# One hybrid decoder layer on one Trainium2 core: scoring in four steps, own token through TensorE, copies of the value results on ScalarE

## The reference

```python
q, k = rms_norm(q, g_q), rms_norm(k, g_k)
gate = einsum(q, mean of k over each block of 256)      # 8 past blocks
idx = top_k(gate, 3)                                     # ties: the lower block first
s_sel = q . k_sel / 8 - slope * distance                 # keys of the three blocks kept
s_own = q . k_own / 8                                    # the sample's own token
p = softmax(concat(s_sel, s_own))
o = p_sel @ v_sel + p_own @ v_own
attn = o @ w_attn_proj
```

## Time and profile before

| | |
|---|---|
| median of 3 runs | 666.08 us (663.58 to 670.77) |
| profiled execution | 667.34 us, span 665.6 us |
| busy in the span: PE, DVE, ACT, POOL | 566.9, 420.4, 240.2, 135.4 us |
| mean granted TensorE clock | 0.922 |

### The profile page before, as it was taken

The page is one execution under the profiler, slowest core; times in us unless marked ns, Lnnn a source line. Parts: engine busy times, 40 slices in busy tenths (PEclk is TensorE's granted clock), DMA queues, the critical chain, the costliest instruction groups (busy, mean ns, idle before and its releaser), DMA issues.

```text
span 665.6 us, 10279 instructions
## 1 busy us (share of the span) xinstructions
PE 566.9 (85%) x4080; PEld 463.0 (70%) x4080; DVE 420.4 (63%) x735; ACT 240.2 (36%) x438; POOL 135.4 (20%) x206
## 2 busy tenths in 40 slices
PE   4869998778778797868679597977999999999997
PEld 2657686546455554536446586966999999999997
DVE  2425793598797979887865366346655666664441
ACT  1102311454462727342135143136433344333341
POOL 8110100274746657661010000000000000000000
PEclk9969998798888887979988899976999999999999
DMA  8998297439896887898472739644775845466600
GB/s 264 384 413 311 73 406 245 160 127 387 285 401 254 348 330 279 342 373 349 162 296 85 261 130 391 225 133 148 232 254 191 286 158 182 120 173 175 176 34 33
DMA packets 85199, 159.30 MB, mean 239 GB/s; under 512 B 2572, under 2 KB 61112, under 8 KB 81047
## 3 DMA queue, kind: packets, MB, share of 16 engines
q1 hardware_dynamic: 79328, 89.27, 40.4%
q0 software_dynamic: 5120, 67.71, 25.7%
q10 hardware_dynamic: 703, 1.67, 0.7%
HBM read 156.39 MB, written 2.72 MB: 239 GB/s over the span
## 4 chain that ended last, share of the span: by engine, by line
PE 61%; DVE 15%; DMA 13%; POOL 4%; ACT 3%; issue 3%; ACTq 1%; SPq 1%; POOLq 0%; DVEq 0%
PE acc L1200 13%; PE acc L1291 12%; PE acc L1292 11%; PE acc L1293 11%; DMA kring<-in_cache_k,rowof 5%; PE chain L1376 4%; DVE prod L819 3%; DVE sall L826 3%; POOL cvT L471 3%; PE acc L1167 3%; DMA wring<-in_w_ada 2%; DMA wring<-in_w_out 2%; DMA wring<-in_w_attn_proj 1%; DMA wring<-in_w_ffn_in 1%; DVE wlo L896 1%
## 5 line engine op out<-in xcount | busy, mean ns | idle before, releaser
L1200 PE MATMUL acc<-hT,wring 128*128 128x264 f32 x576 | 158.8, 430 | 3.7 <-DVE hT L785 1.9
L896 DVE TENSOR_TENSOR wlo<-wring,whi 128x1024 fp32r<-128x1024 f32 (+2 forms) x92 | 101.9, 1108 | 93.2 <-ACT whi L499 92.5
L1200 PEld LDWEIGHTS acc<-hT,wring 128*128 128x128 f32 x576 | 116.5, 210 | 36.7 <-issue 13.5
L1291 PE MATMUL acc<-xlo,whi 128*128 128x264 f32 x416 | 123.9, 298 | 13.5 <-DVE xT L1070 7.4
L499 ACT ACTIVATE whi<-wring 128x1024 fp32r<-128x1024 f32 (+2 forms) x92 | 88.2, 963 | 119.4 <-PE acc L1293 94.3
L1292 PE MATMUL acc<-xhi,wlo 128*128 128x264 f32 x416 | 120.9, 291 | 0.0
L1293 PE MATMUL acc<-xhi,whi 128*128 128x264 f32 x416 | 120.9, 291 | 0.0
L471 POOL TENSOR_TENSOR cvT<-cvT,cprod 128x256 f32<-128x256 f32 x120 | 88.2, 735 | 86.6 <-ACT cprod L499 71.3
L1291 PEld LDWEIGHTS acc<-xlo,whi 128*128 128x128 f32 x416 | 81.2, 195 | 18.2 <-DVE wlo L896 8.6
L819 DVE TENSOR_TENSOR prod<-kring,qbc 128x1024 f32<-128x1024 f32 x64 | 77.4, 1210 | 7.5 <-DMA kring<-in_cache_k,rowof 3.3
L1292 PEld LDWEIGHTS acc<-xhi,wlo 128*128 128x128 f32 x416 | 81.7, 197 | 0.1
(11 more groups left out here) (221 smaller groups left out, 623.5 us busy)
## 6 DMA issues: line engine op xcount, KB each, us to landing
wring<-in_w_ada SPq DMA_DIRECT2D x24, 1024.0 KB, 8.2
wring<-in_w_ffn_in SPq DMA_DIRECT2D x22, 1024.0 KB, 6.8
wring<-in_w_in SPq DMA_DIRECT2D x12, 1024.0 KB, 19.1
wring<-in_w_ffn_out SPq DMA_DIRECT2D x16, 704.0 KB, 5.8
wring<-in_w_out SPq DMA_DIRECT2D x4, 1024.0 KB
wring<-in_w_in SPq DMA_DIRECT2D x6, 512.0 KB, 14.3
wring<-in_w_in SPq DMA_DIRECT2D x4, 768.0 KB, 12.2
wring<-in_w_conv_proj SPq DMA_DIRECT2D x2, 1024.0 KB, 15.7
```

Source lines behind the costliest of these rows:

```text
L896: v.tensor_tensor(wlo[:, place, 0:n, :], w, whi[:, place, 0:n, :].bitcast(F32), ALU.subtract)\
L1200: ins = mm(bank[:, 0:R], w[:, k, P * t:P * t + P], src[:, k, :], start=k == 0, stop=k == KD - 1)
L1291: mm(bank[:, 0:R], whi[:, place, k - k0, :], lo[:, k, :], start=k == 0, stop=False)
```

## The change

It was announced as: scoring in four steps, own token through TensorE, copies behind the value matmuls on ScalarE, value matmuls in the next sample's turn, third key place. The diff does this:

- Scoring goes in 4 steps of 4 pages (`STEPS` = 4), so `multiply` and `add_up` have 2048 elements each; steps 0 and 1 read the first half of the keys, 2 and 3 the second. The steps are placed anew between the softmax steps: step 0 stands ahead of the copy that opens the turn.
- The three comparisons and one sum that rank the blocks become a subtraction and two fused instructions.
- The own token's values go through TensorE: the value rows of the samples are kept as rows (`vrow`, partitions 32 to 39), DVE makes an 8 x 8 weight `pown`, and one more matmul adds it to the value result. The products and sums of the own token on DVE go.
- The weights of the value matmuls are no longer padded (`pg`, 8 columns for 32). The result lies in `chain` alone, which is cleared once; all other small results lie in a bank `small`, and the prompt's output shares a bank with its turned rows.
- ScalarE copies the value result out of PSUM unmasked (`pvm`); the head is chosen by the turned copies, whose second operand is `headof`. ScalarE also writes them to `oT`. Both stand behind the copy of the prompt's output in its queue. TensorE does the turned copies behind the next prompt scores.
- The scalings of the prompt's exponentials move from DVE to ScalarE, behind the second portion of tap products. The ring of tap products has 4 places for 5.
- On TensorE the first gate tile is finished before the turned rows, and the sum of the exponentials stands ahead of the prompt's value matmuls. The query of `b+2` is spread in turn `b`.
- The last turn does the convolution's SiLU and split ahead of the copy of the value result.

```diff
-STEPS = 8
...
-CONV_RING = 5
+CONV_RING = 4
...
+                tap_products(b, 1)
+                act.wait_ge(prin_ready, b + 1)
+                for t, (c0, c1) in enumerate(((0, P), (P, 384))):
+                    func(pr[:, c0:c1], pr[:, c0:c1], ACT.Copy, scale=prin[:, t:t + 1]).then_inc(pn_ready, 1)
                 act.wait_ge(pt_ready, b + 1)
                 act.wait_ge(pp_ready, b)
                 func(prT[:, :], psT[:, 0:384], ACT.Copy).then_inc(pc_ready, 1)
-                tap_products(b, 1)
...
+                if b == B - 1:
+                    conv_rows()
+                act.wait_ge(v_used, CH * (b + 1))
+                func(pvm[:, :], pv[:, :], ACT.Copy).then_inc(pvm_ready, 1)
+                act.wait_ge(pv_ready, b + 1)
+                for e in range(2):
+                    rows = slice(DH * e, DH * e + DH)
+                    func(oT[rows, :, S + b], pvT[rows, e:H:2], ACT.Copy).then_inc(o_ready, 1)
...
+                multiply_next(0)
                 dve.wait_ge(gs_ready, b + 1)
-                v.tensor_copy(gsT[:, :], chain[:, 0:QU]).then_inc(gst_ready, 1)
+                v.tensor_copy(gsT[:, :], sums_).then_inc(gst_ready, 1)
+                add_up_next(0)
...
-                at_same = mark(v.tensor_tensor(cmp1[:, :, :], gm, gn, ALU.is_equal))
-                at_higher = mark(v.tensor_tensor(cmp2[:, :, :], gm, gn, ALU.is_gt))
-                dve.wait_ge(dve_step, at_same)
-                at_first = mark(v.tensor_tensor(cmp1[:, :, :], cmp1[:, :, :], lower[0:H, :, :], ALU.mult))
+                at_less = mark(v.tensor_tensor(cmp1[:, :, :], gm, gn, ALU.subtract))
...
+                dve.wait_ge(dve_step, at_less)
+                at_first = mark(v.scalar_tensor_tensor(cmp2[:, :, :], cmp1[:, :, :], 0.0, lower[0:H, :, :],
+                                                       ALU.is_equal, ALU.mult))
...
+                at_count = mark(v.scalar_tensor_tensor(cmp2[:, :, :], cmp1[:, :, :], 0.0, cmp2[:, :, :],
+                                                       ALU.is_gt, ALU.add))
...
-                multiply_next(0)
+                multiply_next(1)
...
-                add_up_next(0)
...
                 v.tensor_reduce(m1, s1[:, :, :].rearrange("p g h -> p h g"), AX.X, ALU.max).then_inc(m1_ready, 1)
-                multiply_next(1)
+                add_up_next(1)
                 if j == 0 and i + 1 < CT:
                     gated_glu(i + 1)
-                add_up_next(1)
+                dve.wait_ge(pe_ready, 2 * b + 2)
+                v.reciprocal(prin, psum_).then_inc(prin_ready, 1)
...
                 v.tensor_scalar(dg, ident[0:H, 0:H], nmx, None, ALU.mult).then_inc(dg_ready, 1)
-
-                dve.wait_ge(dve_step, at_prin)
-                at_pn = mark(v.tensor_scalar(pr[:, 0:P], pr[:, 0:P], prin[:, 0:1], None, ALU.mult))
-                dve.wait_ge(dve_step, at_pn)
-                v.tensor_scalar(pr[:, P:384], pr[:, P:384], prin[:, 1:2], None, ALU.mult).then_inc(pn_ready, 1)
+                multiply_next(2)
                 if b == B - 1:
                     scale_rows()
                 if b == 6:
                     samples_convolution()
-                multiply_next(2)
-                add_up_next(2)
                 dve.wait_ge(mb_ready, b + 1)
-                v.tensor_tensor(s1[:, :, :], s1[:, :, :], chain[:, 0:H].unsqueeze(1).to_broadcast([P, PG + 1, H]),
+                v.tensor_tensor(s1[:, :, :], s1[:, :, :], spread_max.unsqueeze(1).to_broadcast([P, PG + 1, H]),
                                 ALU.add).then_inc(s2_ready, 1)
...
-                multiply_next(3)
-                add_up_next(3)
+                add_up_next(2)
                 dve.wait_ge(e_ready, b + 1)
...
                 if b == 6:
                     center()
-                multiply_next(4)
-                add_up_next(4)
+                multiply_next(3)
                 dve.wait_ge(tot_ready, b + 1)
-                at_tot = mark(v.tensor_tensor(rinv, chain[:, 0:H], s1[:, PG, :], ALU.add))
+                at_tot = mark(v.tensor_tensor(rinv, spread_sum, s1[:, PG, :], ALU.add))
                 dve.wait_ge(dve_step, at_tot)
                 at_rinv = mark(v.reciprocal(rinv, rinv))
-                multiply_next(5)
                 dve.wait_ge(dve_step, at_rinv)
-                v.tensor_tensor(ppad[:, :, 0:H], s1[:, 0:PG, :], rinv.unsqueeze(1).to_broadcast([P, PG, H]),
+                dve.wait_ge(v_used, CH * b)
+                v.tensor_tensor(pg[:, :, :], s1[:, 0:PG, :], rinv.unsqueeze(1).to_broadcast([P, PG, H]),
                                 ALU.mult).then_inc(p_ready, 1)
-                at_pown = mark(v.tensor_tensor(s1[:, PG, :], s1[:, PG, :], rinv, ALU.mult))
-                add_up_next(5)
+                v.scalar_tensor_tensor(pown, s1[32:32 + B, PG, :], ident[32:32 + B, 32 + b:33 + b], rinv[32:32 + B, :],
+                                       ALU.mult, ALU.mult).then_inc(p_ready, 1)
+                add_up_next(3)
...
-                dve.wait_ge(dve_step, at_pown)
-                for e in range(2):
-                    rows = slice(DH * e, DH * e + DH)
-                    at_own = mark(v.tensor_tensor(own[rows, :], s1[rows, PG, e:H:2], vT[rows, :, S + b], ALU.mult))
-                multiply_next(6)
-                add_up_next(6)
...
-                dve.wait_ge(v_used, CH * (b + 1))
-                v.tensor_tensor(pvm[:, :].rearrange("p (h d) -> p h d", d=DH),
-                                chain[:, :].rearrange("p (h d) -> p h d", d=DH),
-                                headof[:, :].unsqueeze(2).to_broadcast([P, H, DH]), ALU.mult).then_inc(pvm_ready, 1)
-                multiply_next(7)
...
-                dve.wait_ge(pv_ready, b + 1)
-                dve.wait_ge(dve_step, at_own)
-                for e in range(2):
-                    rows = slice(DH * e, DH * e + DH)
-                    v.tensor_tensor(oT[rows, :, S + b], own[rows, :], chain[rows, 0:AT], ALU.add).then_inc(o_ready, 1)
-                add_up_next(7)
...
+                if b + 2 < B:
+                    spread_query(b + 2)
...
+                if b < B - 1:
+                    tile(f"g{first}", mix, 0, hT, k0=4)
+                else:
...
-                pe.wait_ge(pn_ready, b + 1)
-                pe.wait_ge(pc_ready, b)
+                pe.wait_ge(pn_ready, 2 * b + 2)
+                pe.wait_ge(po_ready, b)
+                pe.wait_ge(o_ready, 2 * b)
                 for t in range(3):
                     ins = nc.tensor.transpose(psT[:, P * t:P * t + P], pr[:, P * t:P * t + P], ident[:, :])
                 ins.then_inc(pt_ready, 1)
-                if b < B - 1:
-                    tile(f"g{first}", mix, 0, hT, k0=4)
+
+                pe.wait_ge(es_ready, b + 1)
+                mm(spread_sum, ones[:, :], es, start=True, stop=True).then_inc(tot_ready, 1)
...
-
-                pe.wait_ge(es_ready, b + 1)
-                mm(chain[:, 0:H], ones[:, :], es, start=True, stop=True).then_inc(tot_ready, 1)
...
                     pe.wait_ge(v_full[c], 16 * (b + 1))
                     for g in range(PC * c, PC * c + PC):
                         q = g % 4
-                        ins = mm(chain[32 * q:32 * q + 32, :], ppad[:, g, :], vring[:, g, :],
-                                 start=g < 4, stop=g >= PG - 4)
+                        ins = mm(pv[32 * q:32 * q + H, :], pg[:, g, :], vring[:, g, :], start=g < 4, stop=PG - 4 < g)
+                        if g == PG - 4:
+                            mm(pv[0:H, :], pown, vrow, start=False, stop=True)
                     ins.then_inc(v_used, 1)
...
-                pe.wait_ge(pvm_ready, b + 1)
-                for t in range(AT):
-                    ins = mm(chain[:, t:t + 1], pvm[:, P * t:P * t + P], ones[:, 0:1], start=True, stop=True)
-                ins.then_inc(pv_ready, 1)
...
                     prompt_scores(b + 1)
+
+                pe.wait_ge(pvm_ready, b + 1)
+                for t in range(AT):
+                    ins = mm(pvT[:, 2 * t:2 * t + 2], pvm[:, P * t:P * t + P], headof[:, 2 * t:2 * t + 2], start=True, stop=True)
+                ins.then_inc(pv_ready, 1)
```

More of the change, by code:

```diff
@@ L31 @@
 QU = 4
-STEPS = 8
+STEPS = 4
 PER_STEP = PG // STEPS
@@ L167, in program @@
         gate = sb("gate", [H, NB])
-        cmp1 = sb("cmp1", [H, NB, NB])
-        cmp2 = sb("cmp2", [H, NB, NB])
+        lanes = pvm[:, 0:P]
+        cmp1, cmp2 = (mrow[0:H, 0, 64 * e:64 * e + 64].rearrange("p (m n) -> p m n", m=NB) for e in range(2))
         pen = sb("pen", [H, NB, H])
         tiny = sb("tiny", [P, 64])
-        m1, nmx, dg, es, rinv, own = (tiny[:, 0:8], tiny[0:H, 8:9], tiny[0:H, 16:24], tiny[:, 24:32],
-                                      tiny[:, 32:40], tiny[:, 40:44])
+        m1, nmx, dg, es, rinv, pown = (tiny[:, 0:8], tiny[0:H, 8:9], tiny[0:H, 16:24], tiny[:, 24:32],
+                                       tiny[:, 32:40], tiny[32:32 + B, 40:48])
         pmx, psum_, prin = tiny[:, 48:50], tiny[:, 50:52], tiny[:, 52:54]
```

(32 more changed lines are left out.)

65 lines of the change are left out of this document (25 added, 40 removed).

## The result

The changed kernel takes 687.76 us (median of 4 runs, 687.28 to 691.25), beside 666.71 of the kernel before in the same session: ratio 1.032, 95% interval 1.026 to 1.039. The direction and the mechanism of the loop were right; two terms were not, and the largest miss lies behind the loop.

The account below looks back on a forecast made before the run. A ring through the second key half was to set turns at 32.05 us; the last turn starts 12.4 us later, plus 0.5 behind it: +12.9 on the profiled execution, so 679 us on the median, range 663 to 689.

Parts of the forecast that it names:

- a ring through the second key half: Loop: product 2, exponential, taps, gathers, next product 2; 12.45 + D = 32.05 us, setting the turn.
- the ring through TensorE: Loop: chain from VectorE to TensorE and back; 10.65 + 20.55 = 31.2 us a turn.
- X: Start of product 2, first user of the second key half, put at T+10.65; 327.45 in turn 6.
- T: Start of a turn's first VectorE copy; the next was put at X+20.55, the last at 355.55.
- the five rounds: Loop from X in turn 1 (167.2) to X in turn 6 (327.45), at 32.05 us each.
- D: Time from the first value gather to the second key half landing; taken as 19.6 us, seen between 18.6 and 21.5.
- The own token's matmul: Extra TensorE pass of 512 columns among the value matmuls; between 0 and 1.4 us, taken as 0.5.
- The total of the stretch: TensorE from value matmuls to the next opening copy: 10.8 + 0.5 own token + 0.7 wait for ScalarE = 12.0 us.
- Behind the loop: After the last turn's start: ScalarE waits for turned copies before splitting the fourth weight unit, 0.5 us.
- The LayerNorm sum behind the softmax sum: Turn 6: VectorE idles from X+5.8 to X+9.8, values at X+16.1, last turn starts at X+28.1, 12.4 us later.
- VectorE as the bound: Rival: VectorE's load sets the turn, so 3.5 us leave each of seven turns: -25, 641 us; chance 0.11.
- The own matmul "alone and draining": Rival: own-token matmul costs 1.4 us for 0.5 and delays the second value gather; 34 a turn, 691; chance 0.10.

Follow-up runs that it names:

- the keys last: Gather order of the changed kernel: GpSimd issues the second key half behind the two value halves; the changed kernel takes 687.76 us.
- the keys first: Changed kernel with the second key half gathered ahead of the two value halves; alone 686.87 us, ratio 1.033.
- the same two edits: Own-token matmul moved ahead of the value matmuls, or deleted, in the changed kernel: 693.4 and 687.3 us; with the keys first 675.8 and 668.5.

## Why the prediction was right, and where it was not

**The loop.** The step that carried the forecast, a ring through the second key half beside the ring through TensorE, is shown by two rows of runs: with the keys last, what leaves TensorE comes back as a wait for keys (4.8 us at product 2, 11.6 and 13.6 with 0.95 and 1.9 us a turn less work); with the keys first, the same two edits take 11 and 18 us off. That the keys first gain nothing alone is another thing, the clock, which the forecast had not in it. X in turn 6 was put at 327.45 and came at 327.21, the last T at 355.55 and came at 356.46. So close a hit is in part luck: X in turn 1 came 1.8 us sooner than put (165.40 for 167.2), and the five rounds took 32.4 us each for 32.05. Of the parts, X without its wait for keys is at T+10.54 in turn 3 (10.65), but 10.2 to 11.7 in the others, and the values are at X+8.67 to X+10.24, 9.3 in the mean of turns 1 to 5 (8.55); first value gather 12.2 to 14.0 behind product 2 (12.45); D 18.4 to 19.0 (19.6).

**How the rings share the time.** I let the longer ring set every turn, with a wait for keys in all of turns 2 to 5. Product 2 waits in turns 1, 3 and 6 only, and 1.4 to 2.0 us, not several. The turns with that wait take 32.8 to 33.0 us (turn 6 aside) and those without 31.9 to 32.6: the two rings are within about 1 us of each other, and a turn is set now by one and now by the other.

**The own token's matmul.** Taken at 0.5 us, measured at 1.9: 5.52 us for 3.62, two more passes of 0.9. The Trainium skill (TensorEngine Tiling (Array Packing), Key Properties) says that a change of tiling mode drains the array; the row of the matmul of 8 partitions standing alone for 0.95 us fits that, without telling a drain from a pass of its own. The upper end of 1.4 that I worked out was still too low, as it left out the group that is split. The total of the stretch came out by luck, 11.65 for 12.0, because of a second error: the 5.49 us for the values in the earlier trace rows were at a mean granted clock of 0.66 (window 234.2 to 239.8), where another turn has 3.64 at 1.00. I read a half-clock row as the price of the work. In the changed kernel the clock in that stretch of the middle turns is 1.00:

```profile
239.10:244.70 5.60, 5.57 (x36) 1.06 (x36) 4.57 (x2) 0.51 (x1) 3.88 (x5) 1.00 0.36 117
```

**Behind the loop.** Taken at 0.5 us, measured at 7.0; this is the mis-sized term, and it is most of the distance from 679 to 688. Its parts: +0.8 to the start of the values; +3.6 in the values, 7.2 us for 3.64, of which 1.9 is the own token and the rest clock; +3.1 from their end to the load of w_attn_proj, which waits behind the fourth unit's split (the experiment, with the split earlier, has this load 2.5 us sooner and the end 3.3); less 0.5 after it. The chain "ScalarE waits, the split is late, VectorE waits 6.84, TensorE waits" was named in the prediction, but priced by the wait for the turned copies alone. ScalarE also waits for the values to end, and TensorE does two convolution units before it turns them, so the queue behind it stood 5.7 us. The last turn in the window from its T to the values, and over the values:

```profile
356.50:370.90 14.40, 9.11 (x90) 7.03 (x90) 9.10 (x28) 7.60 (x17) 0.00 (x0) 0.64 0.62 244
370.90:378.10 7.20, 7.19 (x35) 1.17 (x35) 2.14 (x5) 4.76 (x10) 0.00 (x0) 0.76 0.01 2
```

In the kernel before these two stretches have a granted clock of 0.75 and 1.00. Seven turns of the forecast were off by 0.9 us in all (the last T), the part behind them by 6.5.

**Turn 6.** The LayerNorm sum behind the softmax sum was priced nearly as it came: VectorE waited 5.2 us, and the last T came at X+29.25 (28.1). Of the difference 0.8 stands before the values (X+16.9 for 16.1) and 0.3 in the stretch behind (12.3 for 12.0), which has the values at a lower clock, 6.93 us, and no wait for ScalarE.

**The rivals.** VectorE as the bound is refuted: 1.4 us less of it in a turn bought nothing, and the run that gave it the own token's work back is the fastest of all. By the Trainium skill (Perfetto Trace Analysis, Identifying the Most-Contended Engine) the engine of highest occupancy comes first; here the measurement decides against it, since VectorE, at 83% of a turn, stood in waits on both ends of what was taken away. The own matmul "alone and draining" was nearer as a price, 1.4 for the measured 1.9, and wrong as a turn of 34 us, which hung on D near 21.5: D came at 18.4 to 19.0.

**Left open.** Why the clock of the last turns is lower in one kernel than in another was not settled: the rows show longer standing still before them in most cases, not a cause that was varied on its own. With the keys first it was the other way in the loop: TensorE stood still less, and its clock was lower (0.86 for 0.89). So how much of any single edit's result is its own work and how much the clock can only be read from the traces, as above.

## What to carry to other kernels

Where two rings of nearly one length share a loop, an edit that shortens one of them can measure as nothing, or worse; try it together with an edit of the other before it is judged, and compare TensorE's busy time and granted clock, since here the clock took back 6 us of what one edit had gained. Here work moved from an engine that waited to one that didn't was a loss, though it made the instruction count smaller: the four steps were worth keeping here, and the own token was worth moving back. And when a copy moves to another engine's in-order queue, price in the last turn everything that stands behind it there, not only the copy.

## What the runs showed of the hardware

A lone matmul of 8 partitions and 8 columns over 512 columns takes 0.95 us at full clock amid matmuls on four column groups, as long as a pass of four, and splits a group of four in two (5.52 us for 4.57 when it goes first). In one turn standing still for 5.3 us was followed by ten matmuls in 4.76 us for 2.49, at a granted clock of 0.52, so that wait cost more than its length. Less standing still did not always mean a higher clock: with the keys first the same matmuls of turns 1 to 6 were busy 170.0 us for 164.0. A VectorE product or sum of 2048 elements takes 2.28 us, and one of 1024 takes 1.22, so each large one saves 0.16 us over two small ones.
